# The second attention's table of phases in a two-block fp32 transformer kernel on one core: readers placed one phase after their producers

## The chip, the cores and the metric

One core of a Trainium2 chip runs the whole program: TensorE (PE, with its weight loads shown as PEld), VectorE (DVE), ScalarE (ACT), GpSimd (POOL) and SyncE (SP), each with its own in-order queue, joined by semaphores. The metric is the device time of one execution in microseconds, the median of several.

## The reference, cut to what matters

256 tokens of width 2048 pass through two different transformer blocks. The stretch that the change touches is in the second block, between its input projection and its output projection. From `u = rms_norm(x)` the matrix `w_in_2` gives queries, keys, values, gates and a convolution input. In the program, the attention is cut into eight pieces of two query heads each:

```python
s_cmp = q @ k_cmp.T + bias;  p_cmp = masked_softmax(s_cmp)      # 15 compressed keys
s_sel = q @ k_slc.T + bias;  p_sel = masked_softmax(s_sel)      # with 256 tokens: all blocks
s_win = q @ k_win.T + bias;  p_win = masked_softmax(s_win)      # window 512: all tokens
attn = g0 * (p_cmp @ v_cmp) + g1 * (p_sel @ v_slc) + g2 * (p_win @ v_win)
u = depthwise_conv31(a * sigmoid(gate));  conv = silu(layer_norm(u))
x = x + concat(attn, conv) @ w_out
```

## The kernel before

Everything is held transposed (features on the partitions, 256 tokens along the free axis). Each fp32 product is made of three fp32r products: weights and activations are split into a high part (ACT, `wh`) and a low part (DVE, `wl`), and PE multiplies high by high, high by low and low by high. The weights stream from HBM in pieces of at most 128x1024 through four buffers `raw`; such a piece with its matmuls is called a block here (`sub` in the code). In the stretch of this case a block is eight groups of three matmuls. The stretch has 32 blocks. The first 16 (units `ev_v2` 1 and `ev_q2` 1 to 3) were split earlier in the program ("parked") and come back from HBM already split; the other 16 are those of the output projection's convolution rows (`ev_add` 0 to 7), and ACT and DVE split blocks again from the end of `ev_q2` 2 on, about five blocks ahead of PE.

`make_plan` writes one list for all engines, and each engine's program runs down that list and does its own part of every entry. So the order of the list is the order of each queue. Beside the blocks two lanes advance: `side` (attention) and `conv` (the 31-tap convolution of channel group 3, and the LayerNorm `ln` behind it). In the stretch the units are `quick`: a block is issued in two halves, and after each half `side` advances by one phase; `conv` advances after whole blocks, and after each half while the LayerNorm runs or where the output projection starts. Within one entry `conv` comes ahead of `side`, the ends of units (`evac`) ahead of both, and the splits behind.

An attention piece t (0 to 7) runs through fifteen phases 0 to 14. Piece t+1 starts two phases after piece t, where t is even; even pieces use PSUM banks 3 and 4 and the buffers `SX2a`, `PT2a`, `SCMa`, odd ones banks 6 and 7 and `SX2b`, `PT2b`, `SCMb`. The table `ATTN2` (lines 41, 42) says at which phase each step stands on its engine:

- PE: `sc0` scores, `cmp` compressed scores (into the same banks, so it waits until DVE has read `sc0`), `tr0` turns, `o0` values; `sc1`, `tr1`, `o1` the same for the second branch; `trc`, `oc` for the compressed one.
- DVE: `s0`, `s1` read the scores, add the bias and find the minimum (L2536); `ca` reads the compressed scores, `cb` normalises them; `r0`, `r1` take reciprocals and gates; `out` writes the low part of the result.
- ACT: `e0`, `e1` four exponentials with sums; `ce` the compressed one; `p0`, `p1` four scalings; `t0`, `t1`, `tc` copies of the turned matrix from PSUM to `PT2`; `out` the high part of the result.

Bank 7 is shared by the odd pieces and the LayerNorm's matmuls (PE at `ln` phases 0, 4 and 6). `BANK7` lists the pairs of a PE step and the step that reads it; `bank7_taken()` tells whether the odd piece is between them, and `conv` then may hold back `ln`. Where both stand at the same phase, as for all six pairs of the kernel before, it never says so.

Of the kernel before, what the change touches and what calls it, by code (L numbers as in the profile page):

```python
# [37 lines left out]

ATTN2 = dict(sc0=0, cmp=2, tr0=5, o0=6, sc1=7, trc=10, oc=12, tr1=12, o1=14, s0=0, ca=2, r0=2, cb=5, s1=7, r1=9,
             out=14, e0=2, ce=3, p0=3, t0=5, e1=9, tc=10, p1=10, t1=12)
HEAD_END = ATTN2["out"]
QHOLD = 3

# [53 lines left out]
LN_END = 13  # L99
# [43 lines left out]
def stage(name, i, n, late=0, gaps=()):  # L143

    out = [None] * late
    for ph in range(n):
        out.append(ph)
        if ph in gaps:
            out.append(None)
    return (name, i, out)  # L150
# [131 lines left out]
def pieces(us):  # L282


    subs, gb, joins = [], 0, 0
    for n, u in enumerate(us):
        if u.mode not in ("one", "full", "parked") and len(u.banks) % 2 == 0:
            gb += gb % 2
        aside = u.banks == (3, 4)
        b = u.banks[0 if aside else gb % len(u.banks)]  # L290
        gb += not aside
        u.bank, u.turn = b, (0, 1)
        if u.mode not in ("one", "full", "parked"):
            b2 = u.banks[1 if aside else gb % len(u.banks)]
            gb += not aside
            u.turn = (0, 1) if b < b2 else (1, 0)
            u.pair = (min(b, b2), max(b, b2))
            u.bank = None
            u.join = None
            if u.mode != "nat" and u.ev not in ("ev_h", "ev_fin"):  # L300
                u.join = joins
                joins += 1
        for ms in (((u.turn[0],), (u.turn[1],)) if u.mode == "turn" else ((0, 1),)):
            step = NSUB * 256 // (u.nc if len(ms) == 2 else P)
            subs += [(n, ms, k, min(step, u.nk - k)) for k in range(0, u.nk, step)]

    a = next(s for s, x in enumerate(subs) if us[x[0]].rhs == "U2")
    subs[a:a + 8] = subs[a:a + 3] + subs[a + 4:a + 7] + [subs[a + 3], subs[a + 7]]
    return subs
# [12 lines left out]
def make_plan(us):  # L322


    plan = []
    subs = pieces(us)
    side, conv = Lane(plan), Lane(plan)
    for s in range(NRAW):
        plan.append(("fetch", s, 0))
    nf, ns = NRAW, 0  # L330
    for s in range(4):
        plan.append(("seed", s, 0))
        plan.append(("split", s, 0))
        ns += 1
    full = {s for s, x in enumerate(subs) if us[x[0]].mode == "full"}
    parked = {s for s, x in enumerate(subs) if us[x[0]].mode == "parked"}
    quiet = next(s for s, x in enumerate(subs) if us[x[0]].ev == "ev_g1") + 4
    side.extend([stage("sum_x", 0, 4)])

    def side_step():  # L340
        mark = len(plan)
        side.step()
        new = plan[mark:]

        if any(x[0] == "attn2" and x[2] == HEAD_END and x[1] >= 4 for x in new):
            del plan[mark:]
            for x in new:
                if x[0] == "attn2" and x[2] == HEAD_END and x[1] >= 4:
                    while conv.holds("conv31", x[1] // 2):
                        conv.step()  # L350
                plan.append(x)

    def bank7_taken():

        for kind, t, ph in reversed(plan):
            if kind == "attn2" and t % 2:
                return any(ATTN2[a] <= ph < ATTN2[b] for a, b in BANK7)
        return False

    def lead(x):  # L360

        return LEAD if x - NRAW not in full else AFTER_FULL

    held, going, later = [], [], []
    for s, (n, ms, k, c) in enumerate(subs):
        u = us[n]
        p, after = divmod(s - quiet, PARK_EVERY)
        if 0 <= p < len(parked) and after in (0, 3):
            plan.append(("park_in" if after == 0 else "park", p, 0))
        while nf < len(subs) and nf - NRAW < ns:  # L370
            plan.append(("fetch", nf, 0))
            nf += 1
        while ns < len(subs) and ns <= s + lead(ns):
            if ns not in full and ns not in parked:
                plan.append(("split", ns, 0))
            ns += 1
            if nf < len(subs) and nf - NRAW < ns:
                plan.append(("fetch", nf, 0))
                nf += 1
        if k == 0 and (len(ms) == 2 or ms[0] == u.turn[0]):  # L380
            for what in u.before:
                if what == "side":
                    side.drain()
                elif what == "conv":

                    while not conv.left("ln", 2):
                        if not (conv.live and conv.live[0][0] == "ln" and len(conv.live[0][2]) > LN_END - 7 and bank7_taken()):
                            conv.step()
                        side_step()
                else:  # L390
                    side.width = what
        if u.quick:
            plan.append(("sub", s, 0))
            if u.ev == "ev_add" or conv.live and conv.live[0][0] == "ln":
                conv.step()
            side_step()
            plan.append(("sub", s, 1))
        else:
            plan.append(("sub", s, None))
        if k + c == u.nk and (len(ms) == 2 or ms[0] == u.turn[1]):  # L400
            u.end = s + 1
            held.append((s + u.hold, n))
            later.append((s + u.hold, n))
        while going and going[0][0] <= s:
            plan.append(("evac", *going.pop(0)[1:]))
        while held and held[0][0] <= s:
            m = held.pop(0)[1]
            plan.extend(us[m].mid)
            plan.append(("evac", m, 0))
            going += [(s + ph, m, ph) for ph in range(1, us[m].ends)]  # L410
        if not (conv.live and conv.live[0][0] == "ln" and len(conv.live[0][2]) > LN_END - 7 and bank7_taken()):
            conv.step()
        if (s + 1) % u.pace == 0:
            side_step()
        for x in [x for x in later if x[0] <= s]:
            later.remove(x)
            side.extend(us[x[1]].gens)
            conv.extend(us[x[1]].gens2)
    return plan, subs


def hybrid_block_kernel(nc, a, out):
    units = all_units()
    plan, subs = make_plan(units)
    w_at, _ = weight_places(units, subs)

# [307 lines left out]
    for kind, i, ph in plan:  # L734
        if kind == "attn2" and i % 2:
            for part, _ in BANK7:
                if ATTN2[part] == ph:
                    odd = (i, part)
# [206 lines left out]
    def tensor_program(e):  # L945
# [318 lines left out]
        def attn2(t, ph):  # L1264
# [4 lines left out]
            def bank7(part):  # L1269
                if (t, part) in attn2_after:  # L1270
                    e.wait_ge(ln_d.sem, ln_d.at(0, LN_READ[attn2_after[t, part]]))

            def scores(br):
                for hh in range(2):
                    q, k = Q2[hh * 64:hh * 64 + 64, t, :], KD2[hh * 64:hh * 64 + 64, br, j, :]
                    mm(PS[:, S0 + hh, 0:128], q[:, 0:128], k[:, 0:128])
                    tok = mm(PS[:, S0 + hh, 128:384], q[:, 128:256], k[:, 0:256])
                tok.then_inc(pe.sem)
# [18 lines left out]

            if ph == ATTN2["sc0"]:
                bank7("sc0")
# [9 lines left out]
                scores(0)  # L1309
            if ph == ATTN2["cmp"]:  # L1310
                bank7("cmp")
# [5 lines left out]
                tok.then_inc(pe.sem)  # L1317
            if ph == ATTN2["tr0"]:
                bank7("tr0")
# [1469 lines left out]
```

## Time and profile before

| | us |
|---|---|
| median of 3 runs | 2774.45 |
| lowest, highest | 2770.42, 2777.14 |
| the profiled execution | 2776.2 |
| its span, first to last instruction | 2774.1 |
| PE busy in the span | 2721.2 (98%) |
| DVE, ACT busy | 1945.3 (70%), 1405.7 (51%) |

The profile is of one execution. A busy share is a mean over the whole program; what the attention stretch costs is read from windows of it. The stretch lies at 1810 to 1976 us of the span.

### The profile page before, as it was taken

How to read it: one execution, taken by the hardware profiler on the slowest of the kernel's cores; microseconds unless marked ns; L12 is line 12 of the kernel's file. 1: busy time of each engine (PE TensorE's matmuls, PEld its weight loads, DVE VectorE, ACT ScalarE, POOL GpSimd, SP SyncE). 2: the span in 40 equal slices, each digit the busy share in tenths (PEclk: the TensorE clock that was granted, in tenths of full speed). 3: DMA queues.
4: the chain of work that ended last, by engine and by line, in shares of the span. 5: the costliest groups of instructions: out<-in, count | busy, mean ns of one | idle time of the engine just before them, and what ended most of it. 6: DMA issues, size and time to landing. Idle time of an engine off the chain costs nothing. (4 is left out here: it accounts for less than half of the span.)

```text
span 2774.1 us, 41613 instructions
## 1 busy us (share of the span) xinstructions
PE 2721.2 (98%) x16606; PEld 2390.1 (86%) x16606; DVE 1945.3 (70%) x2922; ACT 1405.7 (51%) x2084; POOL 101.5 (4%) x189
## 2 busy tenths in 40 slices
PE   8999999999999999999999998999999999999998
PEld 7888888888888888888888898988888888888887
DVE  7448777757777775677656777876787775677765
ACT  6345555544455554455444551247655553455543
POOL 1320000000000000000000000000000000000000
PEclk9999999999999999999999999999999999999999
DMA  7457556655568878878656566762455556555554
GB/s 239 134 176 240 173 183 197 182 182 191 198 224 290 278 279 301 287 273 279 213 172 205 179 203 232 250 252 92 137 169 193 194 190 192 180 193 194 183 194 141
DMA packets 166609, 573.19 MB, mean 207 GB/s; under 512 B 19872, under 2 KB 26736, under 8 KB 165904
## 3 DMA queue, kind: packets, MB, share of 16 engines
q1 hardware_dynamic: 151216, 521.86, 56.7%
q0 software_dynamic: 15056, 48.65, 4.7%
q8 instruction: 132, 2.16, 0.3%
q14 instruction: 61, 0.50, 0.1%
q10 hardware_dynamic: 144, 0.01, 0.0%
HBM read 530.86 MB, written 38.90 MB: 205 GB/s over the span
## 5 line engine op out<-in xcount | busy, mean ns | idle before, releaser
L1911 DVE TENSOR_TENSOR wl<-raw,wh 128x1024 fp32r<-128x1024 f32 (+1 forms) x880 | 1029.1, 1195 | 449.2 <-ACT wh L1368 447.2
L1368 ACT ACTIVATE wh<-raw 128x1024 fp32r<-128x1024 f32 (+1 forms) x880 | 886.1, 1031 | 508.6 <-PE PS L947 417.0
L947 PE MATMUL PS<-CHt,wh 128*128 128x512 f32 x2816 | 887.2, 396 | 2.5 <-DVE wl L1911 2.5
L947 PE MATMUL PS<-BIGt,wh 128*128 128x512 f32 (+1 forms) x2816 | 757.9, 357 | 2.2 <-DVE wl L1911 1.2
L947 PEld LDWEIGHTS PS<-CHt,wl 128*128 128x128 f32 x2816 | 529.7, 188 | 125.0
L947 PE MATMUL PS<-AHt,wh 128*128 128x512 f32 (+1 forms) x1984 | 602.6, 385 | 12.5 <-DVE wl L1911 9.4
L947 PE MATMUL PS<-CHt,wl 128*128 128x256 f32 x2816 | 554.3, 278 | 0.0
L947 PEld LDWEIGHTS PS<-BIGt,wl 128*128 128x128 f32 x2304 | 436.2, 189 | 79.0 <-issue 0.2
L947 PE MATMUL PS<-BIGt,wl 128*128 128x256 f32 x2304 | 498.9, 279 | 0.0
L947 PEld LDWEIGHTS PS<-BIGt,wh 128*128 128x128 f32 x2816 | 436.4, 191 | 7.1 <-issue 4.4
L947 PEld LDWEIGHTS PS<-CHt,wh 128*128 128x128 f32 x2816 | 430.1, 189 | 3.0 <-issue 2.7
L947 PEld LDWEIGHTS PS<-AHt,wl 128*128 128x128 f32 x1856 | 350.2, 189 | 76.2 <-issue 0.7
L947 PE MATMUL PS<-AHt,wl 128*128 128x256 f32 x1856 | 377.2, 279 | 0.0
L947 PEld LDWEIGHTS PS<-AHt,wh 128*128 128x128 f32 x1984 | 306.3, 189 | 20.0 <-DVE wl L1911 9.4
L1368 ACT ACTIVATE Z<-PS 128x512 f32<-128x512 f32 (+1 forms) x93 | 52.4, 571 | 131.6 <-PE PS L947 131.6
L1911 DVE TENSOR_TENSOR Z<-PS,Z 128x512 f32<-128x512 f32 (+1 forms) x93 | 60.5, 656 | 59.1 <-ACT Z L1368 57.0
L947 PE MATMUL PS<-H,raw 128*128 128x256 f32 x448 | 101.4, 382 | 0.0
L1919 DVE SCALAR_TENSOR_TENSOR CC<-Z,CV,CC 128x256 f32<-128x256 f32 x240 | 97.4, 478 | 0.0
L947 PEld LDWEIGHTS PS<-H,raw 128*128 128x128 f32 x448 | 83.6, 190 | 14.5 <-issue 3.9
L1911 DVE TENSOR_TENSOR H<-H,PS 128x512 f32<-128x512 f32 (+1 forms) x114 | 76.4, 675 | 16.1 <-PE PS L947 14.3
L1368 ACT ACTIVATE BIGt<-TC 128x256 fp32r<-128x256 f32 x88 | 32.0, 410 | 98.6 <-DVE TC L1911 98.6
L1919 DVE SCALAR_TENSOR_TENSOR TA<-Z,CV,TA 128x256 f32<-128x256 f32 x160 | 69.0, 479 | 14.9 <-ACT TA L1368 14.8
(307 smaller groups left out, 1647.1 us busy)
## 6 DMA issues: line engine op xcount, KB each, us to landing
raw<-in_w_up SPq DMA_DIRECT2D x264, 512.0 KB, 4.9
raw<-in_w_in SPq DMA_DIRECT2D x200, 512.0 KB, 4.1
raw<-in_w_down SPq DMA_DIRECT2D x132, 512.0 KB, 4.3
raw<-in_w_gate SPq DMA_DIRECT2D x88, 512.0 KB, 5.3
raw<-in_w_down SPq DMA_DIRECT2D x56, 384.0 KB, 3.6
raw<-in_w_ssd_br SPq DMA_DIRECT2D x32, 512.0 KB, 4.4
raw<-in_w_o SPq DMA_DIRECT2D x32, 512.0 KB, 4.4
PKR<-in_w_in SPq DMA_DIRECT2D x32, 512.0 KB, 5.4
```

Source lines behind the costliest of these rows:

```text
L947: return e.matmul(o, l, r, start=start, stop=stop, skip_group_check=True)
L1368: return e.activation(o, x, f, **k)
L1911: return e.tensor_tensor(o, x, y, op)
L1919: return e.scalar_tensor_tensor(out=o, in0=x, scalar=s, in1=y, op0=o0, op1=o1)
```

## The change

Nine of the 24 entries of `ATTN2` grow by one phase: `s0`, `r0`, `s1`, `r1` on DVE, `p0`, `t0`, `p1`, `t1` on ACT and `o0` on PE. (`s0` 0 to 1, `r0` 2 to 3, `s1` 7 to 8, `r1` 9 to 10, `p0` 3 to 4, `t0` 5 to 6, `p1` 10 to 11, `t1` 12 to 13, `o0` 6 to 7; the other entries stay.) No instruction is added or taken away on any engine; SP's and POOL's queues are the same. `bank7_taken()` can now be true at the odd piece's phases 0, 5, 7 and 12, and a second place in `make_plan` asks it before it advances the LayerNorm.

```diff
-ATTN2 = dict(sc0=0, cmp=2, tr0=5, o0=6, sc1=7, trc=10, oc=12, tr1=12, o1=14, s0=0, ca=2, r0=2, cb=5, s1=7, r1=9,
-             out=14, e0=2, ce=3, p0=3, t0=5, e1=9, tc=10, p1=10, t1=12)
+ATTN2 = dict(sc0=0, cmp=2, tr0=5, o0=7, sc1=7, trc=10, oc=12, tr1=12, o1=14, s0=1, ca=2, r0=3, cb=5, s1=8, r1=10,
+             out=14, e0=2, ce=3, p0=4, t0=6, e1=9, tc=10, p1=11, t1=13)
@@
         if u.quick:
             plan.append(("sub", s, 0))
-            if u.ev == "ev_add" or conv.live and conv.live[0][0] == "ln":
+            if u.ev == "ev_add" or conv.live and conv.live[0][0] == "ln" and not (
+                    len(conv.live[0][2]) > LN_END - 7 and bank7_taken()):
                 conv.step()
             side_step()
             plan.append(("sub", s, 1))
```

The list itself shows what the table and the condition do to the LayerNorm: its phase 2 and its phase 6 are each held back by one half block, so that its phases 2 to 5 come one half block later than before, and 6 to 12 two.

First place: DVE's queue at the first two pieces. `CC_141` and `CC_142` are the convolution's accumulators of channel group 3. Before, from the end of `ca` of piece 0 to the start of `s0` of piece 1:

```order
L1911 TENSOR_TENSOR SCMa<-SCMa,SM 128x30 x2
L1915 TENSOR_SCALAR SM<-SM 128x4
L2542 RECIPROCAL SM<-SM 128x4
L1911 TENSOR_TENSOR SM<-SM,GAT 128x2 x2
L2536 ISA SX2b,SM<-PS,BM 128x128
```

Now (all lines behind the edit stand one further down):

```order
L1912 TENSOR_TENSOR SCMa<-SCMa,SM 128x30 x2
L1916 TENSOR_SCALAR SM<-SM 128x4
L1920 SCALAR_TENSOR_TENSOR CC_141<-Z_144,CV,CC_141 128x256
L1920 SCALAR_TENSOR_TENSOR CC_142<-Z_144,CV,CC_142 128x256
L1920 SCALAR_TENSOR_TENSOR CC_141<-Z_144,CV,CC_141 128x256
L1920 SCALAR_TENSOR_TENSOR CC_142<-Z_144,CV,CC_142 128x256
L1920 SCALAR_TENSOR_TENSOR CC_141<-Z_144,CV,CC_141 128x256
L1920 SCALAR_TENSOR_TENSOR CC_142<-Z_144,CV,CC_142 128x256
L2543 RECIPROCAL SM<-SM 128x4
L1912 TENSOR_TENSOR SM<-SM,GAT 128x2 x2
L2537 ISA SX2b,SM<-PS,BM 128x128
```

One phase of the convolution, six instructions, moved ahead of `r0` and `s0`. `s0` of piece 0 is passed by six such instructions too.

Second place: DVE's queue where piece 2 and the LayerNorm start (`TA` holds the mean, `CC_135` to `CC_142` the eight channel groups' halves). Before:

```order
L1919 SCALAR_TENSOR_TENSOR AHt<-PS,AHt 128x256
L2536 ISA SX2a,SM<-PS,BM 128x128
L2536 ISA SM 128x1
L2536 ISA SX2a,SM<-PS,BM 128x256
L2536 ISA SM 128x1
L2536 ISA SX2a,SM<-PS,BM 128x128
L2536 ISA SM 128x1
L2536 ISA SX2a,SM<-PS,BM 128x256
L2536 ISA SM 128x1
L1915 TENSOR_SCALAR TA<-PS 128x256
L1911 TENSOR_TENSOR CC_135<-CC_135,TA 128x256
```

Now:

```order
L1920 SCALAR_TENSOR_TENSOR AHt<-PS,AHt 128x256
L1916 TENSOR_SCALAR TA<-PS 128x256
L1912 TENSOR_TENSOR CC_135<-CC_135,TA 128x256
L1912 TENSOR_TENSOR CC_136<-CC_136,TA 128x256
L1912 TENSOR_TENSOR CC_137<-CC_137,TA 128x256
L1912 TENSOR_TENSOR CC_138<-CC_138,TA 128x256
L1912 TENSOR_TENSOR CC_139<-CC_139,TA 128x256
L1912 TENSOR_TENSOR CC_140<-CC_140,TA 128x256
L1912 TENSOR_TENSOR CC_141<-CC_141,TA 128x256
L1912 TENSOR_TENSOR CC_142<-CC_142,TA 128x256
L2537 ISA SX2a,SM<-PS,BM 128x128
```

`s0` of piece 2 moved behind the LayerNorm's mean and its eight subtractions.

Third place: DVE's queue at piece 5, where the output projection has begun and a unit's end (`ev_add`, the rows with `H`) stands in the list. Before:

```order
L2542 RECIPROCAL SM<-SM 128x4
L1911 TENSOR_TENSOR SM<-SM,GAT 128x2 x2
L2536 ISA SX2b,SM<-PS,BM 128x128
L2536 ISA SM 128x1
L2536 ISA SX2b,SM<-PS,BM 128x256
L2536 ISA SM 128x1
L2536 ISA SX2b,SM<-PS,BM 128x128
L2536 ISA SM 128x1
L2536 ISA SX2b,SM<-PS,BM 128x256
L2536 ISA SM 128x1
L1919 SCALAR_TENSOR_TENSOR H<-H,CV,RXK 128x256 x2
L1911 TENSOR_TENSOR H<-H,PS 128x512
```

Now:

```order
L1920 SCALAR_TENSOR_TENSOR H<-H,CV,RXK 128x256 x2
L1912 TENSOR_TENSOR H<-H,PS 128x512
L2543 RECIPROCAL SM<-SM 128x4
L1912 TENSOR_TENSOR SM<-SM,GAT 128x2 x2
L2537 ISA SX2b,SM<-PS,BM 128x128
```

`r0` of piece 4 and `s0` of piece 5 moved behind the end of the unit; the same stands at piece 7.

## Rows read from the trace of the kernel before

**Rows 1.** Windows of three stretches: length, busy us (instructions) by engine, PEclk, DMA share, GB/s
```profile
1813.20:1850.09 36.89, 36.89 (x338) 33.18 (x336) 29.12 (x119) 19.19 (x60) 0.00 (x0) 1.00 0.61 223
1850.09:1905.02 54.93, 43.63 (x352) 38.76 (x351) 33.01 (x120) 37.33 (x98) 0.00 (x0) 0.91 0.40 143
1905.02:1976.00 70.98, 70.98 (x648) 64.10 (x648) 49.90 (x183) 50.59 (x131) 0.00 (x0) 1.00 0.35 116
```

**Rows 2.** Waits of PE, 1810 to 1980: us in total, times, longest us
```profile
PE PS L947 <- ACT PT2a L1368: 7.3, 3, 3.3
PE PS L1283 <- DVE CC L1911: 2.1, 1, 2.1
PE PS L947 <- DVE Q L1919: 1.4, 1, 1.4
PE PS L947 <- DVE SCMb L1911: 1.2, 1, 1.2
```

**Rows 3.** Windows of three shorter stretches, for the granted clock
```profile
1870.00:1880.00 10.00, 7.88 (x71) 7.00 (x70) 6.20 (x25) 6.92 (x19) 0.00 (x0) 1.00 0.24 84
...
1886.50:1891.30 4.80, 4.53 (x25) 3.87 (x22) 0.00 (x0) 4.80 (x18) 0.00 (x0) 0.50 0.00 0
...
1897.50:1901.70 4.20, 3.81 (x24) 3.58 (x19) 1.56 (x2) 2.60 (x5) 0.00 (x0) 0.60 0.08 24
```

**Rows 4.** Timeline, pieces 0 and 1: start, duration, engine, line, operation
```profile
1814.59 0.27 DVE L2536 CUSTOM_DVE_ANT_0 SX2a<-PS,BM 128x128 f32<-128x128 f32 x1
...
1815.70 2.45 DVE L1919 SCALAR_TENSOR_TENSOR CC<-Z,CV,CC 128x256 f32<-128x256 f32 x6
...
1816.27 0.62 PE L947 MATMUL PS<-KDC,Q 64*128 64x15 f32 x8
...
1818.08 0.30 DVE L1911 TENSOR_TENSOR SCMa<-PS,CBI 128x30 f32<-128x30 f32 x2
...
1819.06 0.17 DVE L2542 RECIPROCAL SM<-SM 128x4 f32<-128x4 f32 x1
...
1819.41 0.29 DVE L2536 CUSTOM_DVE_ANT_0 SX2b<-PS,BM 128x128 f32<-128x128 f32 x1
...
1820.67 0.62 PE L947 MATMUL PS<-KDC,Q 64*128 64x15 f32 x8
```

**Rows 5.** Timeline, piece 2 and the LayerNorm's start
```profile
1850.22 0.29 DVE L2536 CUSTOM_DVE_ANT_0 SX2a<-PS,BM 128x128 f32<-128x128 f32 x1
...
1853.11 0.42 DVE L1915 TENSOR_SCALAR TA<-PS 128x256 f32<-128x256 f32 x1 [1.69 <-PE PS L947]
...
1853.57 2.77 DVE L1911 TENSOR_TENSOR CC<-CC,TA 128x256 f32<-128x256 f32 x8
...
1854.42 0.62 PE L947 MATMUL PS<-KDC,Q 64*128 64x15 f32 x8
```

**Rows 6.** Timeline, piece 5
```profile
1910.40 0.28 DVE L2536 CUSTOM_DVE_ANT_0 SX2b<-PS,BM 128x128 f32<-128x128 f32 x1
...
1912.41 0.69 DVE L1911 TENSOR_TENSOR H<-H,PS 128x512 f32<-128x512 f32 x1
1912.46 0.52 PEld L947 LDWEIGHTS PS<-KDC,Q 64*128 64x128 f32 x8
```

**Rows 7.** Timeline, the LayerNorm beside pieces 2 and 3
```profile
1863.99 1.28 ACT L1368 ACT_TABLE_LOAD   x1
...
1865.28 0.20 ACT L1368 ACTIVATE TA<-TA 128x2 f32<-128x2 f32 x1
...
1869.39 2.73 DVE L1911 TENSOR_TENSOR CC<-CC,PS 128x256 f32<-128x256 f32 x8
...
1895.43 0.79 ACT L1368 ACTIVATE PT2a<-PS 128x768 f32<-128x768 f32 x1
```

**Rows 8.** Groups of ACT by shape, 1813 to 1976: busy, mean ns | idle before
```profile
L1368 ACT ACTIVATE wh<-raw 128x1024 fp32r<-128x1024 f32 x21 | 22.0, 1049 | 8.1 <-PE PS L947 8.1
L1368 ACT ACTIVATE SX2a<-SX2a,SM 128x256 f32<-128x256 f32 x32 | 15.8, 494 | 0.0
```

## The prediction

> **What bounds the kernel now.** I read the windows first. Attention pieces 0 and 1 run in 36.89 us and pieces 4 to 7 in 70.98 us, and in both PE is busy for the whole stretch [rows 1]. Only in the middle, where the LayerNorm's phases lie between those of pieces 2 and 3, does it stand: 54.93 us with 43.63 busy, 11.3 idle [rows 1]. The list of PE's waits names what it stands for: ACT's copies to `PT2a` 7.3 us in three waits, the LayerNorm's last use of bank 7 2.1, the compressed scores of piece 3 1.2 [rows 2]. (The 1.4 for `Q` lies ahead of these stretches.) The clock windows come next: PE still had the full 2.4 GHz around the 2.1 us wait, but 1.2 GHz from before 1886.50 to 1891.30, after the wait of 3.3, and 1.2 GHz again in most of 1897.50 to 1901.70, after another long one [rows 2, 3]. A PEclk of 0.60 over 4.2 us is 3.4 us at half speed; the first stretch began in the wait that ended at 1886 and held some 5.2 us of work. Half of 5.2 and of 3.4 is 4.3 us lost. So 11.3 + 4.3 = 15.6 us is all that any order of this work could win here, and outside the middle PE has nothing to give back. There a later reader can only cost.
>
> What the change can cost is read from the slack: how long before PE's compressed scores (`cmp`, which overwrite the scores) DVE had read the scores.
>
> **Pieces 0 and 1: +3.3 us.** DVE is nearly full here (29.12 of 36.89) [rows 1]. `s0` of piece 0 started at 1814.59 and took 1.1 to 1.2, to the start of the convolution's phase at 1815.70; PE's `cmp` followed at 1816.27 [rows 4]. Now the convolution's 2.45 us go first [rows 4], so `s0` ends at 1818.2 and PE waits 2.0 us. For piece 1 the path is: `cmp` of piece 0 (0.62), `ca` (1818.08 to 1819.06, 1.0), the six convolution instructions (2.45), `r0` (to 1819.41, 0.35), `s0` (1.2), together 5.6; PE's own work from one `cmp` to the next is 1820.67 - 1816.27 = 4.4 [rows 4]. PE waits 1.2 to 1.3. Behind that `e0`, `p0` and `tr0` keep the distances they have today. Bounds: nothing, if DVE had caught up by then; 4.0, if each handover adds 0.3. The queue was full up to 1820, so I take 3.3.
>
> **Pieces 4 to 7: +1.6 us.** `s0` of piece 5 started at 1910.40, `cmp` at 1912.46 [rows 6]. Now it stands behind the end of a unit, whose addition (0.69) has to wait for the block's last matmul, half a block before 1912.46. Two halves are PE's 4.4 us [rows 4] less the 1.3 of `cmp` and the next `sc0`, so one is 1.5 and the block ended at about 1911.0. Addition, `r0` and `s0` give 1911.0 + 0.69 + 0.35 + 1.2 = 1913.2, and PE waits 0.8. Piece 7 has the same place; the even pieces have nothing between. Two times 0.8; bounds 0 and 2.5. The moved copies, scalings and `s1`, `r1` have a half block or more of slack each, since ACT is busy for only 50.59 of 70.98 [rows 1].
>
> **The middle, without the clock: -1.9 us.** Today `s0` of piece 2 runs at 1850.22, at once. Now it stands behind the mean (1853.11) and the eight subtractions (1853.57 + 2.77 = 1856.3) and ends at 1857.5; PE wants `cmp` at 1854.42 and waits 3.1 us [rows 5]. From there I walked the three queues phase by phase to the end of piece 3, with today's durations: half a block 1.5; four exponentials or scalings 1.5 to 1.8 (0.49 for the longer of each two [rows 8]); a split 1.05 [rows 8]; a copy 0.8 [rows 7]; a LayerNorm step of two channel groups 1.7 to 2.2. The walk gives these waits of PE:
>
> - 3.1 at `cmp` of piece 2, 0.4 at `tr0` and 0.25 at `o0` of piece 2. The 1.2 for the compressed scores is gone, and most of the first of today's waits for `PT2a`.
> - 2.1 at `sc1` of piece 3. The LayerNorm's phase 6 now comes a block later, so `tr0` of piece 3 is free of it, but `sc1`, the next user of bank 7, waits for the same eight products with the root (2.73 us [rows 7]). This is the old 2.1 in a new place.
> - 0.75 at `tr1` of piece 2 instead of 3.3 at `oc`, since `p1` is the last before it and `tc` no longer stands behind the LayerNorm's steps.
> - 5.55 at `o1` of piece 2. ACT's copy for it stood at 1895.43 [rows 7]. In the walk ACT reaches it at about 1894.0: it has the second table load in this queue now and waits 2 us for `trc` of piece 2, but loses less to DVE. PE is there at 1889.1.
> - 1.75 at `o1` of piece 3, whose copy now stands behind the LayerNorm's last step and `out` of piece 2.
>
> The sum is 13.9 us of waits against 11.3, and 54.93 - 11.3 - 4.3 = 39.3 of work at full clock. 39.3 + 13.9 = 53.2, against 54.93: 1.8 to 1.9 us won, all of it from the clock. The bounds are wide, since each wait hangs on the one before: the 15.6 less the sure 3.1 and 2.1 gives -10.4, and 3 us more where two queues meet gives +3.
>
> A rule of the Trainium skill bears on ACT's queue. The row shows the load of an activation table at 1863.99 for 1.28 us and the next operation at 1865.28, with nothing between [rows 7]. The Trainium skill ("ScalarE: Activation LUTs", What ACT_TABLE_LOAD costs) gives 1283 ns and a drain of some 1380 ns more. By it the second load, which the new order puts straight ahead of piece 2's second exponentials, would hold ACT 1.4 us longer and the sum would be 1.2 us higher, as an estimate from that page. The trace agrees with the load's figure and shows no drain, so I leave it out.
>
> **The middle, the clock: +2.6 us.** The walk was at full clock. Both waits of about 3 us or more today had a stretch at 1.2 GHz behind them, and the one of 2.1 had not [rows 2, 3]. The new waits of 3.1 and 5.5 should have one each, of 3.4 to 6.8 us (today's two), which costs half of that, 1.7 to 3.4. After the first, 0.65 is taken up by the two waits that follow: +1.8. After the second, the 1.75 of piece 3 takes most: +0.8.
>
> The Trainium skill ("TensorE: Matmul & The Clock Gate", Part 1) calls the throttled state the default, which activity releases. By that the short waits of 2.0 and 1.3 at pieces 0 and 1 are a risk too; the 2.1 us wait at full clock [rows 2, 3] speaks against it here, and no price for it is in the sum.
>
> **The sum.** 3.3 + 1.6 - 1.9 + 2.6 = 5.6 us. The profiled execution (2776.2) would become 2781.8; it lies 1.75 above the median, and I put the sum on the median: 2774.45 + 5.6 = 2780.05, say 2780.1. A measurement of this kernel tells 0.2% from nothing, which is 5.5 us, so the forecast lies on the edge of slower.
>
> **The rivals.**
>
> - *No fall of the clock behind the wait of piece 2* (0.20): without its 1.8 the sum is +3.8, 2778.3, no change. For it: between 2.1 and 3.3 no wait in these rows tells where the clock holds.
> - *The middle runs free* (0.09, faster). The place is ACT's copy for `o1` of piece 2. If it reached the copy by 1889.1, when PE is there, and with it piece 3's, then 5.55, 1.75 and 0.75 go and the clock stays up: 15.6 - 3.1 - 2.1 = 10.4 won in the middle, less 4.9 outside, is -5.5: 2768.9. For it: the LayerNorm is spread over two half blocks more. Against it: ACT is busy for 37.33 us, and PE has 39.3 of work [rows 1]; for a free run ACT would need a queue with hardly a gap in it.
> - *The new waits compound* (0.15, slower). A LayerNorm step on ACT needs DVE's product, DVE's next split needs ACT's, and a missed turn costs 1 to 3 us; it happens today (piece 2's copies). Two or three more, or clock stretches of 6.8 us, make +8 to +14, 2785.
> - *The delays outside are taken up* (0.11). DVE idles for 7.8 of 36.89 us at pieces 0 and 1 [rows 1]; were that idle time in front of the moved reads, the +4.9 outside would be nearly nothing and the whole within 1 us: 2775.1. Against it: the rows show it full at that moment.
> - The forecast itself has 0.45, from +3.5 to +9, which I split 0.27 slower to 0.18 no change.
>
> **The numbers.** Slower by over 0.2%: 0.27 + 0.15 = 0.42. Within: 0.18 + 0.20 + 0.11 = 0.49. Faster: 0.09. The range leaves out the free run and the end of the compounding: 2771.5 (the taken-up case less the 3 us by which the runs scatter) to 2786.5 (+12).
>
> **What would show each step.** In the profile after: PE waits for DVE's reads (L2537) ahead of `KDC,Q` four or five times: 2.0, 1.3, 3.1, 0.8, 0.8. The wait for `CC` sits at the scores (`KD,Q`), not at the turn. `PT2a` remains the longest wait, in one piece of 5 or more. The stretch from piece 0's start to piece 7's end, 162.8 us today, would be some 168. Wrong would be: no wait at `KDC,Q` for pieces 0 and 1; the sum of the waits in the middle below 8 us; a clock of 1.0 throughout.

## The result, and the profile after

| | us |
|---|---|
| before, median of 12 runs | 2773.95 |
| changed, median of 12 runs | 2781.01 (2776.46 to 2785.01) |
| ratio | 1.0023, 95% interval 1.0015 to 1.0032 |
| the profiled execution, its span | 2781.08, 2778.9 |
| PE busy in the span | 2719.8 (98%) |

The changed kernel is slower by 0.23%, 0.15% at least: 6.4 us by the ratio, 7.1 by the medians. 2780.1 was forecast. PE is busy as before; what the profile shows of the added time is in PE's waits and its clock between 1812 and 1981 us.

The three stretches in the profile of the changed kernel, which answer to [rows 1] (the same columns: length, busy us (instructions) of PE, PEld, DVE, ACT, POOL, PEclk, DMA share, GB/s). Here and below each stretch goes from the first scores (`KD,Q`) of pieces 0, 2 and 4 to the next of these, and the last to the last `o1` of piece 7. Before, that makes 36.89, 54.93 and 71.53:

```profile
1812.21:1851.89 39.68, 36.62 (x336) 33.06 (x336) 29.83 (x120) 18.69 (x59) 0.00 (x0) 1.00 0.57 208
1851.89:1908.15 56.26, 45.46 (x352) 41.07 (x350) 32.81 (x119) 37.44 (x98) 0.00 (x0) 0.85 0.40 145
1908.15:1980.77 72.62, 70.86 (x651) 64.03 (x649) 49.63 (x183) 51.48 (x131) 0.00 (x0) 1.00 0.32 110
```

2.8, 1.3 and 1.1 us longer, 5.2 in all; the other 1.9 of the 7.1 us are not traced. PE now idles outside the middle too (3.06 and 1.76 us), where it never did. Its waits, 1810 to 1985, answer to [rows 2]:

```profile
PE PS L948 <- DVE SM L2537: 7.8, 5, 3.0
PE PS L948 <- ACT PT2a L1369: 5.5, 1, 5.5
PE PS L948 <- DVE CC L1912: 2.0, 1, 2.0
PE PS L948 <- DVE Q L1920: 1.4, 1, 1.4
PE PS L1284 <- ACT SX2a L1369: 0.3, 1, 0.3
```

One line is new, PE waiting for DVE's read of the scores (`SM`, L2537), five times. The same waits one by one, from the timeline of PE; in brackets the idle time just before the row and what ended it:

```profile
1818.06 0.62 PE L948 MATMUL PS<-KDC,Q 64*128 64x15 f32 x8 [1.87 <-DVE SM L2537]
1823.71 0.62 PE L948 MATMUL PS<-KDC,Q 64*128 64x15 f32 x8 [1.19 <-DVE SM L2537]
1860.17 0.62 PE L948 MATMUL PS<-KDC,Q 64*128 64x15 f32 x8 [3.02 <-DVE SM L2537]
1880.91 0.93 PE L948 MATMUL PS<-KD,Q 64*128 64x128 f32 x8 [2.02 <-DVE CC L1912]
1889.15 0.87 PE L1284 MATMUL PS<-M,SX2a 128*128 128x128 f32 x6 [0.26 <-ACT SX2a L1369]
1898.84 1.55 PE L948 MATMUL PS<-PT2a,VN 128*64 128x128 f32 x12 [5.50 <-ACT PT2a L1369]
1917.40 0.62 PE L948 MATMUL PS<-KDC,Q 64*128 64x15 f32 x8 [0.88 <-DVE SM L2537]
1954.82 0.62 PE L948 MATMUL PS<-KDC,Q 64*128 64x15 f32 x8 [0.88 <-DVE SM L2537]
```

Why it waits there stands in DVE's and ACT's rows, from the timeline of all engines. The twelve and six `CC<-Z,CV,CC` are the convolution ahead of `s0` of pieces 0 and 1, the eight subtractions `CC<-CC,TA` are ahead of `s0` of piece 2, and ACT's copy to `PT2a` stands behind the LayerNorm's last steps on `CC`, `TB` and `AHt`:

```profile
1812.07 4.83 DVE L1920 SCALAR_TENSOR_TENSOR CC<-Z,CV,CC 128x256 f32<-128x256 f32 x12
1816.82 0.28 DVE L2537 CUSTOM_DVE_ANT_0 SX2a<-PS,BM 128x128 f32<-128x128 f32 x1
...
1819.73 2.46 DVE L1920 SCALAR_TENSOR_TENSOR CC<-Z,CV,CC 128x256 f32<-128x256 f32 x6
1822.10 0.17 DVE L2543 RECIPROCAL SM<-SM 128x4 f32<-128x4 f32 x1
...
1822.46 0.29 DVE L2537 CUSTOM_DVE_ANT_0 SX2b<-PS,BM 128x128 f32<-128x128 f32 x1
...
1856.23 2.78 DVE L1912 TENSOR_TENSOR CC<-CC,TA 128x256 f32<-128x256 f32 x8
1858.92 0.29 DVE L2537 CUSTOM_DVE_ANT_0 SX2a<-PS,BM 128x128 f32<-128x128 f32 x1
...
1895.80 1.07 ACT L1369 ACTIVATE CC<-CC,CV 128x256 f32<-128x256 f32 x2
...
1897.70 0.40 ACT L1369 ACTIVATE AHt<-TC 128x256 fp32r<-128x256 f32 x1
1898.00 0.78 ACT L1369 ACTIVATE PT2a<-PS 128x768 f32<-128x768 f32 x1
```

The windows in which the granted clock was low, which answer to [rows 3]:

```profile
1862.24:1865.65 3.41, 3.41 (x18) 3.41 (x18) 2.37 (x12) 1.60 (x5) 0.00 (x0) 0.51 0.17 50
1882.70:1886.10 3.40, 3.40 (x18) 3.14 (x17) 1.48 (x8) 1.18 (x3) 0.00 (x0) 0.51 0.44 154
1896.40:1906.60 10.20, 7.76 (x45) 7.10 (x46) 4.43 (x10) 7.56 (x16) 0.00 (x0) 0.50 0.16 53
```

Three windows at 1.2 GHz, 17.0 us with 14.6 us of PE's work in them, one behind or around each wait of 2 us or more in the middle.

### The profile page after: what moved, and what is told of

It reads as the page before. It is cut to its first block and busy times, and to the rows that moved or that the text cites. A ratio compares the mean times of both kernels' runs of the same rounds, so it can differ in the third digit from the quotient of the medians.

```text
span 2778.9 us, 41614 instructions
## 1 busy us (share of the span) xinstructions
PE 2719.8 (98%) x16606; PEld 2389.1 (86%) x16606; DVE 1945.2 (70%) x2922; ACT 1406.3 (51%) x2084; POOL 101.5 (4%) x189
## 5 line engine op out<-in xcount | busy, mean ns | idle before, releaser
L948 PE MATMUL PS<-AHt,wh 128*128 128x512 f32 (+1 forms) x1984 | 602.3, 384 | 13.1 <-DVE wl L1912 10.2
L1912 DVE TENSOR_TENSOR H<-H,PS 128x512 f32<-128x512 f32 (+1 forms) x114 | 76.4, 676 | 15.4 <-PE PS L948 13.4
```

Source lines behind the costliest of these rows:

```text
L948: return e.matmul(o, l, r, start=start, stop=stop, skip_group_check=True)
L1912: return e.tensor_tensor(o, x, y, op)
```

## The experiments

The theory: PE is the bound outside the middle, so a reader of PSUM put behind other work on its queue costs what PE then waits, entry by entry; in the middle the moved entries trade waits, and the clock adds to them. The rivals: the copies on ACT or the values on PE (`o0`) are the price; the middle is an accident of how the queues meet; what is won at one place is lost at the next.

All twelve, each timed against the kernel before on the same chip. The lengths are of the profiled execution; "idle + busy" splits the middle into PE's waits and PE's busy time, of which 39.3 would be the work at full clock by the prediction, the rest what the clock took. The difference in the median is against the median of before measured beside it. All keep the change's second place in `make_plan`; where nothing else is said only entries of `ATTN2` differ. A stretch is read from one execution of a kernel, which lay up to 3.6 us from that kernel's median (e4), so a difference of 1 or 2 us between two middles is weak evidence where no single wait explains it.

The entries also decide through `bank7_taken()` where the LayerNorm stands in the list. Against the kernel before, the list of the changed kernel and of h2 has the LayerNorm's phases 2 to 5 one half block later and the rest two. In e2 all from phase 2 on come one later, in f3 all from phase 6 on one, and in e4 all from phase 1 on one, from phase 5 on two and from 6 on three. In the eight others none is held back. So a run that moves `s0`, or puts it back, changes two things in the middle: the place of the read and the place of the LayerNorm.

| kernel | 0, 1 | middle = idle + busy | 4 to 7 | sum, against before | median, against before | ratio, interval |
|---|---|---|---|---|---|---|
| before | 36.89 | 54.93 = 11.30 + 43.63 | 71.53 | 163.35 | | |
| changed | 39.68 | 56.26 = 10.80 + 45.46 | 72.62 | +5.2 | +7.1 | 1.0023 (1.0015 to 1.0032) |
| e2_s0_alone | 40.31 | 57.07 = 10.46 + 46.61 | 72.89 | +6.9 | +7.3 | 1.0024 (1.0014 to 1.0033) |
| e1_s0_back | 38.46 | 49.36 = 8.32 + 41.04 | 71.21 | -4.3 | -4.9 | 0.9981 (0.9972 to 0.9990) |
| e6_o0_alone | 36.50 | 53.66 = 10.14 + 43.52 | 70.74 | -2.5 | -3.2 | 0.9988 (0.9979 to 0.9997) |
| e3_act_alone | 36.88 | 55.68 = 10.61 + 45.07 | 72.53 | +1.7 | +1.6 | 1.0004 (0.9995 to 1.0013) |
| g2_second_alone | 36.88 | 53.52 = 10.95 + 42.57 | 72.30 | -0.7 | -1.7 | 0.9996 (0.9988 to 1.0005) |
| g1_second_and_o0 | 36.51 | 51.23 = 9.84 + 41.39 | 71.93 | -3.7 | -3.9 | 0.9987 (0.9978 to 0.9996) |
| e4_side_first | 36.50 | 48.19 = 8.17 + 40.02 | 74.46 | -4.2 | -4.3 | 0.9987 (0.9978 to 0.9996) |
| f4_o0_side_first | 36.51 | 54.60 = 8.24 + 46.36 | 70.74 | -1.5 | -1.9 | 0.9990 (0.9981 to 0.9998) |
| f2_first_branch_back | 36.77 | 49.50 = 7.65 + 41.85 | 72.27 | -4.8 | -4.3 | 0.9982 (0.9973 to 0.9991) |
| f3_first_back_side_first | 36.76 | 54.82 = 10.43 + 44.39 | 72.27 | +0.5 | -0.7 | 0.9996 (0.9987 to 1.0005) |
| h2_conv_behind | 36.51 | 58.08 = 11.87 + 46.21 | 72.63 | +3.9 | +3.7 | 1.0013 (1.0004 to 1.0023) |
| h1_s0_back_conv_behind | 36.50 | 49.34 = 8.01 + 41.33 | 71.21 | -6.3 | -5.7 | 0.9979 (0.9971 to 0.9988) |

The stretch accounts for the time: its sum and the difference in the median are at most 1.9 us apart. What lies outside it scatters by some 6 us from one execution to the next (2605.8 of h1's span, 2612.2 of e4's) with no order of its own.

### s0 alone, and s0 put back

The table of before with one entry moved (e2), and the changed table with that entry put back (e1). The LayerNorm's delays come and go with it: one half block in e2, none in e1 where the changed kernel has two:

```diff
-s0=0
+s0=1
```

> The kernel before with s0 alone moved to phase 1 (and the condition on the LayerNorm that it needs). Theory A: the five waits of 1.9, 1.2, 3.0, 0.9 and 0.9 us ahead of KDC,Q appear as in the changed kernel, and it is 5 to 9 us slower than the kernel before. Theory B: within 2 us of the kernel before.

> The changed kernel with s0 alone put back to phase 0. Theory A (what costs is that DVE's first read of the scores stands behind the convolution, the LayerNorm and the ends of units): no wait of PE for L2537 ahead of KDC,Q is over 0.3 us, pieces 0 and 1 take some 36.5 us and pieces 4 to 7 some 70.2 between the starts of their scores; the middle is within 3 us of before, since the wait for ACT's copy at o1 of piece 2 stays at 4 us or more; in all 1.5 us below the kernel before, give or take 3. Theory B (the later copies and scalings on ACT and the later r0, s1, r1 cost): at most 2 of the 6 us over the kernel before go away.

Measured: `s0`, with the delay of the LayerNorm that comes with it, costs 7.3 us, as much as the whole change. Put back, 12.0 come off (+7.1 to -4.9), and what is left of the change is faster than before. PE's waits of e2, from its timeline:

```profile
1816.31 0.62 PE L948 MATMUL PS<-KDC,Q 64*128 64x15 f32 x8 [1.86 <-DVE SM L2537]
...
1859.03 1.04 PE L948 MATMUL PS<-KDC,Q 64*128 64x15 f32 x8 [3.01 <-DVE SM L2537]
...
1954.38 0.62 PE L948 MATMUL PS<-KDC,Q 64*128 64x15 f32 x8 [0.62 <-DVE SM L2537]
```

Four of the five waits are there, and the one behind the unit end at piece 5 (0.63) and at piece 7 (0.62) is shorter than the 0.88 of the changed kernel. The fifth, 1.19 at piece 1, is not: after the first wait PE ran at 1.2 GHz for 3.4 us (the window stands in the last section), which made its work 1.56 us longer (38.45 busy, 36.89 before), so DVE's read was in time. Outside the middle the entry costs 3.4 and 1.4 us in e2. In e1 none of the five waits is there; but one wait is left at piece 0, at its turn, since `r0` and the scalings behind it still stand behind the convolution:

```profile
1823.81 0.88 PE L1284 MATMUL PS<-M,SX2a 128*128 128x128 f32 x6 [1.73 <-ACT SX2a L1369]
```

Theory A of e1 had the cause right and the middle wrong: it expected 36.5, 70.2 and a middle within 3 us of before, with 4 us or more of wait for ACT's copy at `o1` of piece 2. Measured were 38.46, 71.21 and 49.36, with 1.17 at that copy, so the gain of 4.9 us lies beyond its 1.5 give or take 3.

The moved entry costs 2.1 us in the middle where it moves alone (54.93 to 57.07), and 6.9 where the others have moved (49.36 to 56.26). Only the wait of 3.0 for DVE's read at piece 2 is traced to the read itself. How much of the rest is the read and how much the LayerNorm, held back by one half block in the first pair and by two in the second, no run tells apart. The copy for the wait of 5.5 stands behind the LayerNorm's last steps, so the delay is a rival there.

### o0 alone

```diff
-o0=6
+o0=7
```

> The kernel before with only PE's o0 moved to phase 7, beside sc1. Theory A (a side task between two half blocks costs PE some 0.2 us beyond its matmuls, and two side by side pay it once; the trace of the changed kernel shows 0.4 us less than its waits at pieces 0 and 1, and 0.8 less at pieces 4 to 7): 0.2 us per piece, 1.5 us below the kernel before. Theory B (o0's place is free): within 0.5 us.

Measured: 3.2 us faster, where theory A had 1.5. 0.39 comes at pieces 0 and 1 and 0.79 at 4 to 7, where PE never waited; this is theory A's part. The middle is shorter by another 1.3, which it had not. The timeline of PE in the kernel before, from the end of `o0` of piece 4 to `sc1`:

```profile
1917.54 0.51 PE L947 MATMUL PS<-AHt,wh 128*128 128x256 f32 x2
1917.88 0.29 PE L947 MATMUL PS<-AHt,wl 128*128 128x256 f32 x1
1918.01 0.40 PE L947 MATMUL PS<-AHt,wh 128*128 128x256 f32 x2
1918.24 0.28 PE L947 MATMUL PS<-AHt,wl 128*128 128x256 f32 x1
...
1918.96 0.28 PE L947 MATMUL PS<-AHt,wl 128*128 128x256 f32 x1
1919.17 0.93 PE L947 MATMUL PS<-KD,Q 64*128 64x128 f32 x8
```

and of e6_o0_alone, where `o0` stands right ahead of `sc1`:

```profile
1917.37 0.28 PE L948 MATMUL PS<-AHt,wl 128*128 128x256 f32 x1
1917.58 0.88 PE L948 MATMUL PS<-PT2a,VN 128*64 128x128 f32 x12
1918.39 0.93 PE L948 MATMUL PS<-KD,Q 64*128 64x128 f32 x8
```

Inside the block a `wl` follows its `wh` pair after 0.23 us and a `wh` the `wl` after 0.13. The first pair behind the attention takes 0.34, and an attention step starts 0.21 behind the last `wl`. Turning aside from a block to scores or values cost PE 0.11 + 0.08 = 0.19 here; with `o0` beside `sc1` there is one turn less per piece: 0.38 for two pieces, 0.76 for four. The prediction had put `o0` at nothing.

### ACT's four entries alone

```diff
-p0=3, t0=5, p1=10, t1=12
+p0=4, t0=6, p1=11, t1=13
```

> The table of before with only ACT's four entries moved (p0=4, t0=6, p1=11, t1=13); o0, s0, r0, s1, r1 stay. Theory A (the price of the change is DVE's: readers of the scores put behind other work; the copies and scalings on ACT have slack): no wait of PE at pieces 0, 1 and 4 to 7, stretches 36.9 and 71.5 as before, with up to 0.5 more where o0 now stands right behind its copy; the middle within 2 us of 54.9, for the LayerNorm shifts by a half block; median 2772 to 2776. Theory B (the moved ACT steps cost as much as DVE's, since o0 must now wait for t0 in the same phase): PE waits for PT2a or PT2b some 0.3 to 1 us at each of eight values steps, stretches 38 and 74, median 2778 or more.

Measured: 1.6 us slower, with an interval that includes no change. 36.88 at pieces 0 and 1, and 72.53 instead of 71.53 at 4 to 7, with waits for `PT2a` at `o0` of pieces 4 and 6 of 0.43 and 0.46 us. Theory A holds in the main, with its margin of 0.5 us at pieces 4 to 7 overrun (1.0): these four entries are not the price of the change, though a copy in the same phase as its reader is not free either. The LayerNorm does not shift in this kernel's list, as the expectation had it.

### The second branch alone, and with o0

```diff
-s1=7, r1=9, p1=10, t1=12
+s1=8, r1=10, p1=11, t1=13
```

> The table of before with only the second branch moved (s1=8, r1=10, p1=11, t1=13); o0 stays at 6. Theory A: the same middle as with o0=7 or up to 1.3 us more, 36.9 and 71.5 outside, median 2768.5 to 2770. Theory B: the middle 54 to 57, median 2773.5 to 2776.

> The table of before with o0=7 and only the second branch moved (s1=8, r1=10, p1=11, t1=13); s0, r0, p0, t0 stay. Theory A (o0 costs nothing as long as its copy t0 stands two phases ahead of it, and the second branch's shift is what gives the short middles of 49 us): no wait at pieces 0, 1 and 4 to 7, stretches 36.5 and 70.7 us; the middle 49 to 51; median 2767 to 2768.5, the best of all. Theory B (the short middle needs the first branch's copy t0 moved too, as in both kernels that had it without the attention ahead of the LayerNorm): the middle 53 to 56, median 2771 to 2774.

Measured: alone the second branch does nothing that can be told (-1.7), and its middle of 53.52 and median of 2773.09 fit theory B better than A. With `o0` it is 3.9 us faster, with a median of 2770.84 just below theory B's range. Its middle of 51.23 lies between the two theories' values, and pieces 4 to 7 took 71.93, not 70.7: PE waits 0.17 and 0.28 at the second turns of each pair, and 0.9 behind piece 7. Alone `o0` and the second branch shorten the middle by 1.3 and 1.4 us, together by 3.7, in one execution each.

### The attention ahead of the other lane

The changed kernel with the order within an entry turned round (e4, below). h2 has the second of the two places alone, and there only while `conv` is not yet in the LayerNorm:

```diff
         if u.quick:
             plan.append(("sub", s, 0))
+            side_step()
             if u.ev == "ev_add" or conv.live and conv.live[0][0] == "ln" and not (
                     len(conv.live[0][2]) > LN_END - 7 and bank7_taken()):
                 conv.step()
-            side_step()
@@
+        if u.quick:
+            side_step()
         if not (conv.live and conv.live[0][0] == "ln" and len(conv.live[0][2]) > LN_END - 7 and bank7_taken()):
             conv.step()
-        if (s + 1) % u.pace == 0:
+        if not u.quick and (s + 1) % u.pace == 0:
             side_step()
```

> The changed table, but in every entry with half blocks the attention's phase stands ahead of the convolution's and the LayerNorm's. Theory A: the waits of 1.9, 1.2 and 3.0 ahead of KDC,Q go, the two of 0.9 (behind the ends of units) stay; ACT's copy for o1 of piece 2 no longer stands behind the LayerNorm step of its entry, so its wait falls from 5.5 to 3.5 or less; in all 1 to 5 us below the kernel before. Theory B: no faster than 4 us above the kernel before.

> The changed kernel; only, while the convolution is still running (pieces 0 and 1), the attention's phase goes ahead of the convolution's in the list; the LayerNorm and the unit ends keep their place, and so do all later stretches. Theory A (the first term of the sum stands by itself: the 1.9 and 1.2 us at pieces 0 and 1 are the six convolution instructions ahead of s0, and nothing later depends on them): 36.5 us instead of 39.7 at pieces 0 and 1, both waits for DVE's reads there gone, the middle 56.3 with its wait of 3 us at piece 2, pieces 4 to 7 72.6; median 3.2 below the changed kernel, 2777.5 to 2778. Theory B (what is won here is lost again in the middle, since DVE comes to the mean later with the convolution's last instructions behind the attention): the middle 58 or more, median 2780 or more.

Measured: in both, pieces 0 and 1 take 36.5 us and their waits for DVE's reads are gone. In h2 the difference falls from +7.1 to +3.7, 3.4 less where theory A had 3.2, so the first term of the prediction stands by itself. Its middle is longer than the changed kernel's by 1.8, of which 1.1 is waits (2.55 and 0.81 us where there were 2.02 and 0.26), so a part of theory B is true of that execution, though not of the median. e4 is 4.3 us faster than before, as theory A had it. Its middle idles for 8.2 us instead of 10.8: the copy for `o1` of piece 2 is waited for 0.95 instead of 5.50, but one of 4.03 for `o1` of piece 3 is new. Of the waits for DVE's reads the two of 0.88 behind the unit ends are left, which the edit does not reach, and one of 1.2 is new. Of its 74.46 at pieces 4 to 7, 1.9 are the end of a stretch at 1.2 GHz that began in the middle (the window stands below).

### Towards the best order

`f2` puts back `s0`, `r0` and `p0` in the changed table; `f3` adds the order of e4 to it; `f4` is e6 with the order of e4; `h1` is h2 with `s0=0`:

```diff
-s0=1, r0=3, p0=4
+s0=0, r0=2, p0=3
```

> The table of the changed kernel with the first branch's scores, reciprocals and scalings put back (s0=0, r0=2, p0=3); t0=6, o0=7 and all of the second branch stay moved. Theory A (each reader costs what it stands behind, and nothing else): the 1.73 us wait at the turn of piece 0, which appeared with s0 alone put back, goes, pieces 0 and 1 take 36.5 us, pieces 4 to 7 70.7 to 71.2, the middle stays near 49.4; median 2767.5, below both kernels. Theory B (the short middle was an accident of how that order met the LayerNorm): the middle is back at 53 to 56 and the median at 2771 to 2774.

> The same table, and in addition the attention's phase goes ahead of the convolution's and the LayerNorm's in the list wherever a block is issued in two halves. Theory A (readers of PSUM cost what they stand behind, so with the attention ahead of the eight-channel steps PE waits least): pieces 0 and 1 36.5 us, middle 48 to 50, pieces 4 to 7 71; median 2767 or less. Theory B (a LayerNorm step that is put back is late for bank 7 and for the output projection): a wait of 2 to 4 us for CC or TA appears in the middle or a wait for the convolution's split rows behind piece 7, the middle is 52 or more; median 2770 or more.

> The table of before with o0=7 and the attention's phase ahead of the convolution's and the LayerNorm's. Theory A (the gain of the two middles of 48 and 49 us comes from the order of attention against LayerNorm, not from the moved second branch): pieces 0 and 1 36.5 us, middle 48 to 50, pieces 4 to 7 70.7; median 2767. Theory B (it comes from the second branch's one-phase shift, which gives ACT room): the middle stays near the 53.7 of o0 alone; median 2771.

> The same, and s0=0. Theory A (s0 and the order against the convolution each take their own waits away, and the middle of 49.4 us that the changed table has with s0=0 does not depend on either): 36.5, 49.4 and 71.2 us; median 2767.5, the best version. Theory B (the middle depends on when DVE and ACT come to it, so a change ahead of it moves it by several us): the middle is outside 48.5 to 50.5, median 2769 or more.

Measured: f2 is as fast as e1, not 2 us faster. The 1.73 us at piece 0 is gone (36.77), but PE waits for `PT2a` at `o0` of pieces 4 and 6, 0.57 and 0.81 us, 0.18 at that of piece 0 and 2.29 at that of piece 2. f3 fails theory A: 54.82 in the middle, with a wait of 5.38 for `PT2a`; the middle and the median (2773.19) are theory B's, though its wait of 2 to 4 us for `CC` is only 0.59. f4 fails it too; its 54.60 and 2771.95 are near theory B's 53.7 and 2771. It shows most beside e4: its waits in the middle add up to the same (8.24 and 8.17), yet it is 6.4 us longer there. The windows of low clock of f4_o0_side_first,

```profile
1863.90:1870.60 6.70, 5.51 (x26) 5.54 (x27) 2.32 (x11) 2.41 (x5) 0.00 (x0) 0.51 1.00 407
1887.90:1891.30 3.40, 3.40 (x19) 3.40 (x17) 0.50 (x4) 3.40 (x14) 0.00 (x0) 0.50 0.30 123
1894.90:1901.70 6.80, 6.45 (x39) 5.79 (x40) 4.79 (x9) 4.90 (x11) 0.00 (x0) 0.51 0.38 92
```

and the only one of e4_side_first, which reaches into piece 4:

```profile
1896.10:1902.90 6.80, 5.59 (x32) 4.61 (x33) 5.23 (x16) 3.18 (x7) 0.00 (x0) 0.50 0.26 83
```

15.4 us of PE's busy time at 1.2 GHz against 5.6, of which 4.1 lie behind the middle. So the 6.4 us are the clock, and the longest waits do not tell it: f4's are 3.17 and 2.74, e4's 2.04 and 4.03. Over all three stretches the two executions are only 2.7 us apart, and the differences of their medians to before 2.4, since e4 pays at pieces 4 to 7 for the end of its low stretch and for two waits. The two also differ in their tables and in where the LayerNorm stands.

h1 does what theory A said to 0.1 us: 36.50, 49.34, 71.21, median 2767.50 (2764.96 to 2770.68). Its waits of PE, 1810 to 1985:

```profile
PE PS L1287 <- ACT SX2a L1372: 3.3, 1, 3.3
PE PS L951 <- ACT PT2a L1372: 3.2, 3, 1.5
PE PS L951 <- DVE Q L1923: 1.4, 1, 1.4
PE PS L951 <- DVE SCMb L1915: 1.1, 1, 1.1
PE PS L1287 <- DVE CC L1915: 0.5, 1, 0.5
```

Against [rows 2]: the copies to `PT2a` 3.2 instead of 7.3 us, the shared bank 0.5 instead of 2.1, a new 3.3 at the second turn of piece 2, and no wait outside the middle but that for `Q`. This order beats both kernels: 0.21% under before (0.12 to 0.29), and by its difference to before 12.8 us under the changed one. It keeps eight of the nine moved entries, leaves `s0` where it was, and holds the LayerNorm back nowhere.

## Why the prediction was right

The time was forecast at 2780.1 and measured at 2781.01, on the slower side of the edge as forecast. The mechanism is as the prediction had it: reads of the scores put behind other work, and the clock behind the waits. That the time is met to 0.9 us is in part luck. The kernel before measured 2773.95 beside it and not 2774.45, so +7.1 stands against +5.6; the profile accounts for 5.2 of it; and in that 5.2 two terms forecast 0.5 too high stand against a middle forecast 0.6 too low. The chances also put a little more on no change (0.49) than on slower (0.42).

- **Pieces 0 and 1, +3.3: right, +2.8.** The waits were 1.87 and 1.19 where 2.0 and 1.2 to 1.3 stood. Two turns of PE less, from `o0`, gave 0.4 back. h2 took this term out: 3.4 us of the median went.
- **Pieces 4 to 7, +1.6: right, +1.1.** 0.88 at each of pieces 5 and 7 for 0.8, less 0.8 from `o0`. That `s0` is what costs here is shown by e1, where both are gone.
- **The middle, -1.9 for waits: the large ones were right.** 3.02 for 3.1, 2.02 for 2.1, 0.26 for 0.75, 5.50 for 5.55. The 0.4 and 0.25 at `tr0` and `o0` of piece 2 and the 1.75 at `o1` of piece 3 aren't there, which fits the clock term: it had the slowed PE arrive late enough for 0.65 and for the 1.75. Its own figures give 54.93 - 53.2 = 1.7 and not 1.9, so the sum should have been 5.8; and the low end of its range is 2774.45 less 3, not 2775.1 less 3 as it says. The second table load lies ahead of piece 2's second exponentials, and the walk had ACT's next operation follow it at once. On ACT's timeline 0.40 us lie between, which the profile puts on DVE's read, far less than the 1.4 us that the prediction had left out of its sum:

```profile
1876.29 1.28 ACT L1369 ACT_TABLE_LOAD   x1
1877.97 0.40 ACT L1369 ACTIVATE SX2a<-SX2a,SM 128x128 f32<-128x128 f32 x1 [0.40 <-DVE SM L2537]
```

- **The clock, +2.6: under-sized.** The step that was off is "The new waits of 3.1 and 5.5 should have one each, of 3.4 to 6.8 us", with none behind 2.1. The runs showed three, 3.4, 3.4 and 10.2 us; the one at 1882.70 stands behind the wait of 2.02, which the prediction had taken from [rows 2, 3] to be short enough. The three held 3.41 + 3.40 + 7.76 = 14.6 us of PE's work. By half that is 7.3 us lost, by the 1.56 us that the window of 3.4 cost in e2 6.7, and PE's busy time in the middle stands 45.46 - 39.3 = 6.2 above the prediction's work at full clock, which does not have the turns that `o0` saves. The prediction's two stretches cost 1.8 and 0.8, and 0.65 and 1.75 of waits beside that, 5.0 in all.
- **The middle as a whole:** +0.7 forecast, +1.3 measured.
- **Left out:** that `o0` beside `sc1` saves PE a turn, 0.19 us a piece, 1.2 outside the middle. So "outside the middle PE has nothing to give back" was wrong: PE was busy there all the time and still became 1.2 us faster in e6. By luck this nearly cancels the under-sized clock.

Of the rivals, none came true: the clock fell behind piece 2's wait, the middle did not run free, the delays outside were not taken up, and the waits did not compound. What the prediction did not see is that the rest of the change is a gain: it walked through the changed order alone, and in e1 the middle of the same table with `s0` put back, and with the LayerNorm no longer held back, is 6.9 us shorter, 2.5 in waits and 4.4 in PE's busy time. The risk that it named for the clock behind the short waits at pieces 0 and 1 did not come in the changed kernel and did in e2.

What stays open: why the low stretches come or stay away behind waits of the same length, and so why f4's middle is 6.4 us longer than e4's; and what the LayerNorm's delay costs by itself. No run here separates the waits from the clock, and the only one that holds the LayerNorm back with `s0` in its old place, f3, also turns the order round.

## What to carry to other kernels

Where one engine is full, look in the other engines' queues at what stands ahead of each read that frees its buffer: moving such a read by one phase costs the work that it is put behind, less the slack, and both are in the timeline of before (here five waits, each within 0.15 us). Move producers' and readers' entries one at a time when a table of them is changed, since one bad entry can hide the gain of the rest: the change without its ninth entry was worth 4.9 us, the ninth cost 12.0. Look also at what else in the list an entry moves, as the LayerNorm here. Steps of another kind on a full TensorE are worth trying side by side (0.19 us a piece here), and a stretch in which it waits again and again should be judged by idle time and clock apart, as waits of the same sum gave middles 6.4 us apart.

## What the runs showed of the hardware

The clock's answer to a wait is not fixed. In the changed kernel the 1.87 us wait that ended at 1818.06 left it at 2.4 GHz, as PEclk 1.00 of the first stretch shows. In e2_s0_alone the wait of 1.86 us at the same place was followed by this window:

```profile
1817.80:1821.20 3.40, 3.40 (x17) 3.40 (x18) 3.22 (x14) 1.98 (x7) 0.00 (x0) 0.52 0.00 0
```

1.2 GHz for 3.4 us, from 1.5 us after the end of the wait on. From the scores of piece 0 to the wait PE had done the same in both (4.0 us of work in 5.8). In the 52 us ahead of that it was busy for 50.27 us in e2 and for 49.27 in the changed kernel, so the clock fell in the busier of the two. Low windows of 3.4, 6.8 and 10.2 us occurred. The runs of one kernel follow it: of the changed kernel's twelve, the one with a mean clock of 0.994 took 2776.46 us, one with 0.990 took 2784.74, and a line through all twelve gives 2.05 us more for each 0.001 of clock less.
